# Odd mixer's input in three doubles of seven products, and the mLSTM scan fed with its m rows by transfers

## The reference, cut to what matters

```
q, k, v, o, g, d = split(h @ w_in)        # 512 columns each, g has 16
i_pre, log_f     = gates(g)               # per direction and head
# per direction, over chunks of 128 tokens, with C, n, m carried:
b     = cumsum(log_f);  m_t = max(b + m, max(b - b' + i))
a     = exp(log_d - m_t) * (q . k);       w_prev = exp(b + m - m_t)
num   = a @ v + w_prev * (C @ q);         den = sum(a) + w_prev * (n . q)
h     = num / max(|den|, exp(-m_t))
C, n  = w_p * C + sum(w_s v k'),  w_p * n + sum(w_s k)
out   = concat(sigmoid(o) * (h_f + h_b), fft2(d).real) @ w_out
```

## Time and profile before

| what | us |
|---|---|
| median of 3 runs (2333.28 to 2334.16) | 2333.32 |
| span of the profiled execution, first to last instruction | 2332.0 |
| PE busy | 2315.6 (99%) |
| DVE busy | 1570.3 (67%) |
| ACT busy | 949.1 (41%) |

### The profile page before, as it was taken

The page is one execution under the profiler, slowest core; times in us unless marked ns, Lnnn a source line. Parts: engine busy times, 40 slices in busy tenths (PEclk is TensorE's granted clock), DMA queues, the critical chain, the costliest instruction groups (busy, mean ns, idle before and its releaser), DMA issues.

```text
span 2332.0 us, 39464 instructions
## 1 busy us (share of the span) xinstructions
PE 2315.6 (99%) x16468; PEld 2236.7 (96%) x16468; DVE 1570.3 (67%) x2385; ACT 949.1 (41%) x1491; POOL 30.6 (1%) x44
## 2 busy tenths in 40 slices
PE   8999999999999999999999999999999999999999
PEld 8999999989789999999999999999999999999999
DVE  6886776658867876776587777676245768467473
ACT  5433423444656523414364243245215355234142
POOL 0000000000001000000010000000000010000000
PEclk9999999999999999999999999999999999999999
DMA  9352544422101344334224344225221012322132
GB/s 301 127 163 96 190 148 145 166 70 64 48 19 55 105 149 140 114 109 156 86 91 157 115 156 152 85 78 173 90 73 46 19 55 73 109 73 91 56 99 73
DMA packets 203194, 251.58 MB, mean 108 GB/s; under 512 B 13106, under 2 KB 180874, under 8 KB 203018
## 3 DMA queue, kind: packets, MB, share of 16 engines
q1 hardware_dynamic: 202594, 248.89, 32.5%
q10 hardware_dynamic: 424, 0.18, 0.0%
HBM read 245.76 MB, written 3.28 MB: 107 GB/s over the span
## 4 chain that ended last, share of the span: by engine, by line
PE 91%; DVE 3%; ACT 2%; DMA 2%; issue 1%; SPq 1%; POOL 0%; DVEq 0%; ACTq 0%
PE banks L1111 80%; PE banks L1264 1%; PE banks L1443 1%; PE banks L1442 1%; PE banks L1441 1%; DMA w_raw<-ffn_w_in 1%; PE banks L1588 1%; PE banks L1600 1%; PE banks L1615 1%; DMA mod_first<-w_mod 1%; SPq L1072 0%; SPq L879 0%; PE banks L1809 0%; DVE w_lo L2658 0%; ACT w_hi L2041 0%
## 5 line engine op out<-in xcount | busy, mean ns | idle before, releaser
L1111 PE MATMUL banks<-b_hi,w_hi 128*128 128x320 f32 x2496 | 775.8, 311 | 2.9 <-DVE b_lo L2833 1.2
L1111 PE MATMUL banks<-b_hi,w_lo 128*128 128x320 f32 x2496 | 771.2, 309 | 0.0
L1111 PE MATMUL banks<-b_lo,w_hi 128*128 128x320 f32 x2496 | 771.2, 309 | 0.0
L1111 PEld LDWEIGHTS banks<-b_hi,w_hi 128*128 128x128 f32 x2496 | 468.5, 188 | 15.8 <-issue 9.6
L2041 ACT ACTIVATE w_hi<-w_raw 128x1024 fp32r<-128x1024 f32 x296 | 310.4, 1056 | 403.2 <-PE banks L1111 228.9
L1111 PEld LDWEIGHTS banks<-b_lo,w_hi 128*128 128x128 f32 x2496 | 468.6, 188 | 0.0
L1111 PEld LDWEIGHTS banks<-b_hi,w_lo 128*128 128x128 f32 x2496 | 468.6, 188 | 0.0
L2658 DVE TENSOR_TENSOR w_lo<-w_raw,w_hi 128x1024 fp32r<-128x1024 f32 x296 | 361.4, 1223 | 152.1 <-ACT w_hi L2041 150.6
L1111 PE MATMUL banks<-hid_hi,w_hi 128*128 128x320 f32 x1664 | 400.1, 311 | 0.5 <-DVE hid_lo L2962 0.5
L1111 PE MATMUL banks<-hid_lo,w_hi 128*128 128x320 f32 x1664 | 396.2, 309 | 0.0
L1111 PE MATMUL banks<-hid_hi,w_lo 128*128 128x320 f32 x1664 | 396.2, 309 | 0.0
(11 more groups left out here) (343 smaller groups left out, 2409.6 us busy)
## 6 DMA issues: line engine op xcount, KB each, us to landing
w_raw<-ffn_w_in SPq DMA_DIRECT2D x176, 512.0 KB, 4.8
mod_grain<-w_mod SPq DMA_DIRECT2D x78, 512.0 KB, 6.0
w_raw<-ffn_w_out SPq DMA_DIRECT2D x64, 512.0 KB, 4.4
last_grain<-w_mod SPq DMA_DIRECT2D x40, 512.0 KB, 5.2
w_raw<-ffn_w_out SPq DMA_DIRECT2D x32, 384.0 KB, 3.6
w_raw<-w_in_odd SPq DMA_DIRECT2D x20, 512.0 KB, 4.7
mod_first<-w_mod SPq DMA_DIRECT2D x6, 1024.0 KB, 11.8
w_raw<-w_in_even SPq DMA_DIRECT2D x12, 512.0 KB, 5.8
```

Source lines behind the costliest of these rows:

```text
L1111: ins = pe.matmul(o, w3[w], v3[v][cols], start=first and i == 0, stop=last and i == 2, skip_group_check=onto_read)
```

## The change

Three things are joined.

1. k, d and o are computed as three doubles of seven products (`odd_item`), with the inputs' four sums made once (`sum_form`, `sum_high`, `sum_low`). q stays as two units, v as two. The gate steps are set behind single items.
2. The m rows are written to DRAM once (`m_all`) and read back spread over 128 partitions by a transfer per group into one of five `w_prev` tiles; `bcast` is gone. Numerators of odd n get banks 0 and 1, so a group's numerators no longer wait for the finish of the group before.
3. The order of the prologue and of the scan's iterations is another, `finish` at the first visit moves to ACT, and two `exponents` of ten become one instruction.

```diff
@@ PE: seven products, and the gate steps behind them
+                def odd_item(d, t):
+                    pe.wait_ge(lo_ready, in_ev(ODD, d, t) + 1)
...
+                        for k in range(HK):
+                            ins = split_product([(role(d, s, ITEM_ROLE[t]), slice(None))],
...
+                def turn_starts():
+                    pe.wait_ge(gate_dve, 5)
+                    pe.transpose(bank[7][0:GR, 0:P], m_start[:, :], ident[:, :]).then_inc(gate_pe, 1)
+                behind = {(1, 0): turn_gates, (1, 3): sum_gates, (1, 6): turn_exponents, (2, 2): turn_tops, (3, 0): turn_starts}
@@ PE: prologue and scan
+                pe.transpose(bank[2][:, GR:2 * GR], m_rows[:, 1, :], ident[0:GR, 0:GR]).then_inc(m_turned, 1)
                 token_transform(0)
                 context_transform()
-                bcast(0)
-                bcast(1)
                 token_transform(1)
-                bcast(2)
+                keys_queries(0)
                 token_transform(2)
-                keys_queries(0)
                 token_transform(3)
+                keys_queries(1)
+                numerators(0)
                 for n in range(NG):
+                    if n + 2 < NG:
+                        keys_queries(n + 2)
                     if n + 1 < NG:
-                        keys_queries(n + 1)
-                    numerators(n)
-                    if n + SETS < NG:
-                        bcast(n + SETS)
+                        numerators(n + 1)
                     states(n)
@@ SP: the m rows
+                sp.dma_start(m_all[:, :], m_rows[:, 0, :]).then_inc(rows_out, 16)
+                sp.wait_ge(rows_out, 16)
+                sp.wait_ge(w_used, OV + 1 + 1)
+                for n in range(PREV_SETS - 1):
+                    load_m(n)
...
+                    if n >= PREV_SETS:
+                        sp.wait_ge(a_ready, n - PREV_SETS + 1)
+                        sp.wait_ge(st_taken, n - PREV_SETS + 1)
@@ SP: q goes by a transfer to its place once the sums that lie there are used
+                sp.dma_start(q_f[:, :, :], q_early[:, :, :]).then_inc(q_moved, 16)
@@ ACT: between the last double and the spectra (OV, OV+1: v's units; OO: first of the output)
+                gate_outputs()
+                split(OV + 1)
+                split(OO)
                 for n in range(0, UV, 2):
@@ ACT: scan
+                for n in range(NG):
+                    if not SEEN[n]:
+                        finish_first(n)
+                    if n + SETS < NG:
+                        weights(n + SETS)
+                        values(n + SETS)
@@ DVE: a double
+                def double_of_odd(d):
...
+                    if more:
+                        item_lo(ODD, d + 1, 2)
+                        weight_sum(ODD, d + 1, 2)
+                        if d == 2:
+                            starts_of_tiles()
+                        item_lo(ODD, d + 1, 3)
@@ DVE: between the last double and the spectra
+                quarter_sums()
+                split(OV + 1)
+                dve.wait_ge(q_moved, 16)
                 for t in range(TT):
                     keep_v(t)
+                split(OO)
@@ DVE: prologue and scan
+                for n in range(SETS):
+                    exponents(n)
                 token_low(0)
...
-                exponents(0)
-                exponents(1)
                 token_low(1)
-                split(11)
-                exponents(2)
                 weigh(0)
                 token_low(2)
+                split(OO + 1)
                 token_low(3)
                 for n in range(NG):
                     if n + 1 < NG:
                         weigh(n + 1)
                     invert_den(n)
-                    finish(n)
+                    if SEEN[n]:
+                        finish_second(n)
                     if n + SETS < NG:
                         exponents(n + SETS)
                     update_state(n)
```

More of the change, by code:

```diff
@@ L1049, in odd_sp @@
+                load_m(PREV_SETS)
+                load_mix(OO + 3, wo, KT, slice(768, 1024))
+                for n in range(PREV_SETS + 1, NG):
+                    load_m(n)
                 for d in range(2):
@@ L1770, in odd_pe, with sum_gates @@
-                feature_pair(OU + 7, 10)
-                pe.wait_ge(gate_dve, 5)
-                pe.transpose(bank[2][0:GR, 0:P], m_start[:, :], ident[:, :]).then_inc(gate_pe, 1)
-                feature_pair(OU + 8, 12)
-                feature_pair(OU + 9, 14)
+                def sum_gates():
+                    pe.wait_ge(gate_dve, 2)
+                    for d in range(2):
+                        pe.matmul(bank[4][:, 32 * d:32 * (d + 1)], masks[:, 2 + d, :], log_f[:, 32 * d:32 * (d + 1)],
+                                  start=True, stop=True)
+                    pe.matmul(bank[4][:, GR:2 * GR], ones[:, :], log_f[:, :], start=True, stop=True).then_inc(gate_pe, 1)
@@ L2551, in values, with finish_first @@
                         ins.then_inc(v_ready, 1)
+                def finish_first(n):
+                    t, _ = GROUPS[n]
+                    act.wait_ge(den_ready, n + 1)
+                    if n > 0:
+                        act.wait_ge(h_done, n)
+                    for h in range(CH):
+                        ins = act.activation(h_tok[:, t, h, :], nd_of(n, h)[:, 0:P], ACT.Copy, scale=den[:, n % 2, h:h + 1])
+                    ins.then_inc(h_done, 1)
+                act.wait_ge(m_turned, 1)
+                act.activation(e_m[:, :], bank[2][:, GR:2 * GR], ACT.Exp, scale=-1.0).then_inc(e_m_ready, 1)
                 token_high(0)
+                weights(0)
                 act.wait_ge(four_ready, 2)
@@ L3356, in odd_dve, with split @@
             def odd_dve():
-                def split(i):
-                    split_lo(OU + i, "mix")
-                def keep(f):
-                    odd_tile_ready(dve, f)
-                    dst, scale = (k_f, DK ** -0.5) if f < 8 else (d_f, 1.0)
-                    for hf, cols in halves():
-                        ins = dve.tensor_scalar(dst[:, f % 4, cols], bank[odd_bank(f) + hf][:, 0:HALF], scale, None, ALU.mult)
-                    ins.then_inc(tile_kept_dve, 1)
+                def split(unit):
+                    split_lo(unit, "mix")
                 def keep_v(t):
@@ new lines, in starts_of_tiles @@
+                def starts_of_tiles():
+                    dve.wait_ge(gate_pe, 4)
+                    a_top = bank[4]
+                    for d in range(2):
+                        start = TT - 1 if d else 1
+                        do(dve.tensor_copy(col_view(m_start, d, start), m_given[:, d, :]))
+                        order = [start + (-i if d else i) for i in range(TT - 1)]
+                        for t, nxt in [(0, None)] + list(zip(order[:-1], order[1:])):
+                            top = gate_abs[:, 0, 0, :]
+                            do(dve.tensor_tensor(top, col_view(m_start, d, t), col_view(a_top, d, t), ALU.max))
+                            dst = m_end[:, d, :] if nxt is None else col_view(m_start, d, nxt)
+                            do(dve.tensor_tensor(dst, top, col_view(log_f, d, t), ALU.add))
+                    dve.tensor_copy(gate_abs[:, 1, 0, :], gate_abs[:, 0, 0, :]).then_inc(gate_dve, 1)
@@ L3432, in odd_dve @@
-                keep(8)
-                keep(9)
-                dve.wait_ge(gate_pe, 4)
-                a_top = bank[1]
-                for d in range(2):
-                    start = TT - 1 if d else 1
-                    do(dve.tensor_copy(col_view(m_start, d, start), m_given[:, d, :]))
-                    order = [start + (-i if d else i) for i in range(TT - 1)]
-                    for t, nxt in [(0, None)] + list(zip(order[:-1], order[1:])):
-                        top = gate_abs[:, 0, 0, :]
-                        do(dve.tensor_tensor(top, col_view(m_start, d, t), col_view(a_top, d, t), ALU.max))
-                        dst = m_end[:, d, :] if nxt is None else col_view(m_start, d, nxt)
-                        do(dve.tensor_tensor(dst, top, col_view(log_f, d, t), ALU.add))
```

726 lines of the change are left out of this document (464 added, 262 removed).

## The result

The changed kernel takes 2353.82 us, the median of four runs (2350.96 to 2357.13), against 2333.74 for the kernel before on the same chip (2333.28 to 2335.47): ratio 1.0086, interval 1.0073 to 1.0098. It is slower, as forecast, but by 20 us and not by 6; 2353.8 lies outside the range of 2330 to 2347. The profiled execution took 2355.57 us with a span of 2353.8.

A forecast was written before the change was run, and what follows sets the result against it. TensorE, 99% busy, was taken to bound the kernel, with DVE nearly full too in the scan. Products -10.6, third double's wait +2.0, prologue +1.4, scan +13.0 sum to +5.8: 2333.3 becomes 2339.1 us, range 2330 to 2347.

The forecast's parts named there:

- the sum of the scan: From weigh(1) to weigh(9): 28.6 us of matmuls plus 8 x 2.56 makes 49.1 against 36.1 before, a loss of 13.0.
- The clock: Rival, 9%: TensorE's clock falls to half in the scan; 2368 if throughout, 2347 if through its first two iterations.
- The turn-taking: In the scan PE and DVE alternate (weigh, 32 matmuls, update_state, weigh), adding 2.56 us a turn beside PE's work.
- The wait in the third double: Behind item (3,0), turn_starts waits for the chain of the starts of m; PE stands 2.0 us, bounds 0 and 4.
- The prologue: From v's last product (T) to weigh(1)'s end: T+29.2 against T+27.8 before, a loss of 1.4 us, bounds -3 and +4.
- PE without a wait through doubles 1 and 2: Sign to look for in the changed kernel's timeline: no wait of PE in the first two seven-product doubles.
- the first double's weights: In the tightest double, weights ready about 2 us early; if that cover is gone, it costs 1 to 3 us.
- The gain of the products: k, d and o have 504 matmuls in place of 576; 72 x 0.147 = 10.6 us less on PE.

The follow-up runs named there:

- unread_fitting: The changed kernel with unread matmuls in PE's scan waits, 15 ahead of iteration 0 and 11 behind states(n) (the full fill): 2345.77 us, ratio 1.0047.
- rows_earlier: The changed kernel with states(n) first in each scan iteration and ACT copying gate_rows before rounding item 3 of the first double: 2326.98 us.
- unread_in_waits: The changed kernel with unread matmuls in PE's scan waits, 30 ahead of iteration 0 and 22 behind states(n): 2367.92 us, ratio 1.0150.
- unread_first: The changed kernel with 15 unread matmuls ahead of scan iteration 0 only, none behind states(n): 2355.27 us (2346.91 to 2356.85), ratio 1.0085.

## Why the prediction was right in kind and wrong in size

- **The failed step is the sum of the scan,** where PE's work is entered as "256 x 0.112 = 28.6": 0.112 us is the price of a matmul at full clock, and I carried it into a scan in which I myself had PE stand 2.6 us of every 6.1. In the changed kernel PE was busy 40.6 us for the same 256, and the stretch took 59.96 us. With the waits filled it took 49.94, so the clock is 10.0 of the missing 10.9, and 0.8 is the true length of a turn (6.26 against 6.14).
- **The clock was a rival, at 9%.** Its price was bracketed, 8 us for two iterations and 29 for all; the measured 10 lies between, nearer the small end. I held it unlikely since "the profile of before has no such stretch after its start". That is no evidence: a kernel whose PE never stands can't show what standing costs. The one row there was, 0.20 us a matmul behind 6.4 us of idling, spoke for it by its pace, though not by its granted clock, which the profile of before has at 1.00 there (5 to 17 us). The Trainium skill (TensorE: Matmul & The Clock Gate, section HAM oscillation) tells of a kernel that waits for transfers between bursts of matmuls, and whose array falls back to half its clock at each of these waits. The trace agrees in kind, with waits for DVE (0.80 mean over the scan), but not at each: two of the eight turns ran at 1.00.
- **The turn-taking was right**: place, order and size. PE's idle time is released by a_t nine times, 23.3 us in all, 2.4 each but for the first, of 3.9.
- **The wait in the third double was right in place and near in size**: 1.6 us by PE's waits, 1.88 between two starts, against 2.0.
- **The prologue was right**: DVE's first copy of a spectrum starts 4.41 us behind T (forecast 4.4), weigh(1) ends at T + 29.11 (forecast 29.2). That this trace met full clock there was luck: in five others the same prologue took 30.8.
- **"PE without a wait through doubles 1 and 2" was wrong.** I had said that the first double's weights would be ready 2 us early, and looked at the weights only. What was late is the copy of the gate rows, queued on ACT behind item 3's rounding, which waits for DVE. It cost 2.0, and about 1.5 more by the clock (14 products in 3.59 us in place of 2.06). Small waits for k_f and a weight sum make 0.6 to 1. With the third double's 1.6 to 1.9 that accounts for the -4.1 measured where -8.6 was forecast.
- **The gain of the products was right**: 9.8 of 10.6 once the waits were gone.
- **Open:** 1.9 us behind the scan, where nothing was changed. 1.4 of it are three waits of PE for DVE's `work` in FFN 3, of which the profile of before has none. The same waits are 0.3 us in unread_fitting and 2.6 in rows_earlier, so they come and go between executions; what sets them off isn't shown. The stretch takes 502.2 to 505.2 us in the traces of the experiments, and 505.9 in unread_in_waits, where the end of the last fill stands in it.

## What to carry to other kernels

When a change makes PE wait on another engine in turns, price its matmuls at half clock in the high bound and ask which is likelier; that the profile of before shows a full clock says nothing on it. Before adding a lookahead on PE, look at what stands behind the step that waits: here numerators(n+1) ahead of states(n) held up the very engine it waited for, and swapping them gave back 23 us. Where a wait can't be removed, some unread matmuls in it can pay for themselves, if they fit: 22 a turn cost 14 us, 11 or 5 gained 8.

## What the runs showed of the hardware that I had not expected

- Five unread matmuls in each turn's wait kept the granted clock at 1.00 from the second turn on (0.97 over the scan), with PE still standing 1.3 us of every 6.3 (2345.1 us against 2345.8 with the full fill).
- Equal turns do not meet equal clocks: in unread_first one run passed four turns with stands of 2.4 us at 1.00 before it fell, and the three other runs of the same kernel took 8 to 10 us longer.
- A wait of 2.3 us between two starts in the midst of products, PE busy on both sides, was followed by half clock 1.4 us after it had ended; one of 1.9 us, 54 us later, was not. In four other traces the same first wait was not followed by it either.
- Stands of 0.9 and 1.7 us among short bursts at the start of the prologue were followed by half clock in five of ten traces (30.8 us in place of 29.1).
- A matmul of 128 by 128 by 128 in fp32 stands in the trace as two instructions of 0.112 us each.
